# Attention scores with the keys on the partitions, and a maximum from the high halves alone

## The reference

```python
s = jnp.einsum('bqhd,bkhd->bhqk', qn, k_nope) + jnp.einsum('bqhd,bkd->bhqk', qr, k_rope)
pr = jax.nn.softmax(s.astype(jnp.float32) * scale, axis=-1).astype(v.dtype)
return jnp.einsum('bhqk,bkhd->bqhd', pr, v)
```

## Time and profile before

| | us |
|---|---|
| median of 3 runs | 1148.6 (1147.55 to 1149.5) |
| the profiled execution | 1144.88 |
| its span in the profile | 1143.1 |
| PE busy | 1117.8 (98%) |
| DVE busy | 826.1 (72%) |
| ACT busy | 555.4 (49%) |
| POOL busy | 464.2 (41%) |

### The profile page before, as it was taken

How to read it: one execution, slowest core, us unless ns; L and a number is a source line. 1 busy time by engine, 2 the same in 40 slices (tenths; PEclk the granted TensorE clock), 3 DMA queues, 4 the chain that set the end, 5 groups by cost and what they waited for, 6 DMA issues and landing times.

```text
span 1143.1 us, 15837 instructions
## 1 busy us (share of the span) xinstructions
PE 1117.8 (98%) x5146; PEld 896.6 (78%) x5146; DVE 826.1 (72%) x1170; ACT 555.4 (49%) x986; POOL 464.2 (41%) x405
## 2 busy tenths in 40 slices
PE   8999999999999989999999999999999999999996
PEld 7787766665888867888888888888888888888885
DVE  7784976674468899878787878787876757757555
ACT  6312687775223454545454545454554545533332
POOL 0185642322566046765676567655310202211000
PEclk9999999999999999999999999999999999999999
DMA  6610000104652126444544454445896565533341
GB/s 209 222 44 26 1 12 13 38 19 164 204 202 104 56 81 205 165 138 152 178 165 138 154 176 165 138 155 172 330 344 204 190 197 192 168 108 118 92 143 74
DMA packets 138431, 161.60 MB, mean 141 GB/s; under 512 B 8755, under 2 KB 105354, under 8 KB 133770
## 3 DMA queue, kind: packets, MB, share of 16 engines
q1 hardware_dynamic: 138080, 160.82, 42.0%
q10 hardware_dynamic: 298, 0.11, 0.0%
HBM read 115.55 MB, written 45.35 MB: 141 GB/s over the span
## 4 chain that ended last, share of the span: by engine, by line
PE 86%; DVE 10%; issue 2%; ACT 1%; POOL 1%; DMA 0%; DVEq 0%; SPq 0%; POOLq 0%; ACTq 0%
PE ps L298 26%; PE ps L299 26%; PE ps L300 26%; PE ps L869 2%; PE ps L850 2%; DVE WL L2050 1%; PE ps L711 1%; PE ps L861 1%; DVE XL L1727 1%; DVE SF L2149 1%; DVE SF L2157 1%; DVE WDHL L1907 1%; DVE col L1918 1%; DVE XT L1721 0%; DVE R L1900 0%
## 5 line engine op out<-in xcount | busy, mean ns | idle before, releaser
L298 PE MATMUL ps<-XH,WH 128*128 128x512 f32 x722 | 287.1, 398 | 0.8 <-DVE WL L339 0.5
L300 PE MATMUL ps<-XH,WL 128*128 128x512 f32 x722 | 281.2, 390 | 0.0
L299 PE MATMUL ps<-XL,WH 128*128 128x512 f32 x722 | 281.1, 389 | 0.0
L298 PEld LDWEIGHTS ps<-XH,WH 128*128 128x128 f32 x722 | 135.6, 188 | 32.4 <-issue 3.0
L299 PEld LDWEIGHTS ps<-XL,WH 128*128 128x128 f32 x722 | 135.7, 188 | 29.1 <-issue 2.2
L300 PEld LDWEIGHTS ps<-XH,WL 128*128 128x128 f32 x722 | 135.5, 188 | 28.5
L298 PE MATMUL ps<-GHL,WH 128*128 128x512 f32 x394 | 153.6, 390 | 0.8 <-DVE WL L2050 0.7
L300 PE MATMUL ps<-GHL,WL 128*128 128x512 f32 x394 | 153.3, 389 | 0.0
L299 PE MATMUL ps<-GHL,WH 128*128 128x512 f32 x394 | 153.3, 389 | 0.0
L334 ACT ACTIVATE WH<-WR 128x1024 fp32r<-128x1024 f32 (+3 forms) x45 | 45.5, 1011 | 138.7 <-PE ps L300 129.4
L1476 ACT ACTIVATE SF<-ps,col 128x512 f32<-128x512 f32 x88 | 68.2, 778 | 74.6 <-PE ps L300 65.6
(11 more groups left out here) (241 smaller groups left out, 2250.8 us busy)
## 6 DMA issues: line engine op xcount, KB each, us to landing
TL<-in_w_up SPq DMA_DIRECT2D x48, 256.0 KB, 3.6
s_scratch<-XT SPq DMA_DIRECT2D x11, 1024.0 KB, 4.7
XT<-in_w_down SPq DMA_DIRECT2D x11, 1024.0 KB, 6.5
t_scratch<-XT SPq DMA_DIRECT2D x11, 1024.0 KB, 3.8
WR<-t_scratch SPq DMA_DIRECT2D x44, 256.0 KB, 2.7
TL<-s_scratch SPq DMA_DIRECT2D x44, 256.0 KB, 2.9
WR<-in_w_up SPq DMA_DIRECT2D x40, 256.0 KB, 3.5
WR<-in_w_down SPq DMA_DIRECT2D x33, 256.0 KB, 3.7
```

The source lines that it names most:

```text
L298: pe.matmul(out, wh, xh, start=first, stop=False, skip_group_check=skip)
L299: pe.matmul(out, wh, xl, start=False, stop=False, skip_group_check=skip)
L300: return pe.matmul(out, wl, xh, start=False, stop=last, skip_group_check=skip)
```

## The change

The scores are made the other way round: `scores(v)` now takes 128 keys as weights and all 512 queries of the head as the moving operand. The exponentials then lie as `weigh` needs them, and ACT writes them to `XT` directly (`exponent`); the transposes, their copies and the row sums that came with the exponential are gone. The maximum of a query must be known before the first score: `rough(v)` makes a product of the high halves alone for 128 queries (one product, two banks), DVE takes its negated row maximum into `MXR`, `turn_max(n)` turns the four columns of a head into four rows with one small product, and `max_rows(n)` writes them, each masked to its own block of queries, into four more rows of `QH` (4 x 512). These rows meet ones in `KH` in the first of the three exact products, which so has 100 contraction rows. PE's step is now: `rough` of block v + 3, `scores` of block v - 2, and after every second of four steps `turn_max`.

The sums of the exponentials are added up over the four key blocks on POOL (`key_sum`, three additions per head into `SUM`); PE adds them over the partitions (`total`); DVE transposes the result in blocks of 32 x 32, takes the inverse of 16 columns, ACT spreads it over 32 columns each, DVE transposes back and scales (`inverse`, `spread_rc`, `scale_rows`). The projections and the other work are moved to other steps. POOL writes a rounded identity and the rows of ones once, early in the program. The first of the reloads of `XT` on SP also wait for the sums' product.

```diff
-            def scores(i, u):
-                j, t = divmod(u, TT)
-                s, h = divmod(j, 2)
+            def rough(v):
+                n, t = divmod(v, TT)
+                s, h = divmod(n % 4, 2)
                 if t == 0:
-                    pe.wait_ge(q_lo, i * 4 + j + 1)
-                    pe.wait_ge(k_lo, i * 4 + j + 1)
-                if i * 16 + u >= 3:
-                    pe.wait_ge(exp_done, i * 16 + u - 2)
-                tok = slice(t * P, (t + 1) * P)
-                ins = mm3(pe, s_bank(i * 16 + u)[:, :], QH[0:HEAD, s, h, tok], QL[0:HEAD, s, h, tok],
-                          KH[0:HEAD, s, h, :], KL[0:HEAD, s, h, :], True, True)
-                ins.then_inc(s_ready, 1)
-
-            def turn(i, u):
-
-                pe.wait_ge(exp_done, i * 16 + u + 1)
-                if i == 0 and u < 2:
-                    pe.wait_ge(v_copied, u + 1)
+                    pe.wait_ge(q_hi, n + 1)
+                    pe.wait_ge(k_hi, n + 1)
+                if v >= 2:
+                    pe.wait_ge(max_ready, v - 1)
+                pe.matmul(m_bank(v)[:, :], QH[0:HEAD, s, h, t * P:(t + 1) * P], KH[0:HEAD, s, h, :],
+                          start=True, stop=True).then_inc(m_ready, 1)
+
+            def turn_max(n):
+
+                pe.wait_ge(max_ready, 4 * n + 4)
+                if n:
+                    pe.wait_ge(max_row, n)
                 else:
-                    pe.wait_ge(pt_ready, i * 16 + u - 1)
-                for k in range(TT):
-                    ins = pe.transpose(ps[4 + u % 2][:, k * P:(k + 1) * P], p_buf(i * 16 + u)[:, k * P:(k + 1) * P], ident[:, :])
-                ins.then_inc(p_tr, 1)
+                    pe.wait_ge(k_lo, 2)
+                    pe.wait_ge(consts_set, 4)
+                pe.matmul(ps[1][0:TT, 0:P], MXR[:, n % 2, 0:TT], ident_r[:, :], start=True, stop=True).then_inc(max_turned, 1)
+
+            def scores(v):
+                n, k = divmod(v, TT)
+                s, h = divmod(n % 4, 2)
+                if k == 0:
+                    pe.wait_ge(max_row, n + 1)
+                    pe.wait_ge(q_lo, n + 1)
+                    pe.wait_ge(k_lo, n + 1)
+                if v < 2:
+                    pe.wait_ge(v_copied, v + 1)
+                else:
+                    pe.wait_ge(exp_done, v - 1)
+                keys = slice(k * P, (k + 1) * P)
+                o = s_bank(v)[:, :]
+                pe.matmul(o, KH[0:MAXED, s, h, keys], QH[0:MAXED, s, h, :], start=True, stop=False)
+                pe.matmul(o, KH[0:HEAD, s, h, keys], QL[0:HEAD, s, h, :], start=False, stop=False)
+                pe.matmul(o, KL[0:HEAD, s, h, keys], QH[0:HEAD, s, h, :], start=False, stop=True).then_inc(s_ready, 1)
 
...
+            def total(i, s):
+
+                pe.wait_ge(sum_step, 3 * (i * 4 + 2 * s + 2))
+                if i or s:
+                    pe.wait_ge(rr_copied, i * 2 + s)
+                pe.wait_ge(v_copied, i * 2 + s + 1 + (i < HEADS // 2 - 1) * (2 - s))
+                for h in range(2):
+                    ins = pe.matmul(ps[7][h * V_DIM:(h + 1) * V_DIM, :], ones[:, 0:V_DIM], SUM[2 * s + h], start=True, stop=True)
+                ins.then_inc(rr_ready, 1)
+
             def pair(i, last):
                 for u in range(4 * TT):
-                    turn(i, u)
-                    if u + 3 < 4 * TT:
-                        scores(i, u + 3)
-                    elif not last:
-                        scores(i + 1, u + 3 - 4 * TT)
+                    v = 4 * TT * i + u
+                    if v + 3 < 2 * HEADS * TT:
+                        rough(v + 3)
+                    if v >= 2:
+                        scores(v - 2)
+                    if u % TT == 1:
+                        turn_max(v // TT)
...
-            for u in range(3):
-                scores(0, u)
+            for v in range(3):
+                rough(v)
...
-            def exponent(i, u):
-
-                act.wait_ge(max_ready, i * 16 + u + 1)
-                if i and u % 8 == 0:
-                    act.wait_ge(rc_ready, i * 2 - 1 + u // 8)
-                act.activation(p_buf(i * 16 + u), s_bank(i * 16 + u)[:, :], ACT.Exp,
-                               bias=col[:, NB + u % 4:NB + u % 4 + 1],
-                               accum_out=col[:, RS + u:RS + u + 1]).then_inc(exp_done, 1)
-
...
+            def exponent(v):
+
+                n, k = divmod(v, TT)
+                act.wait_ge(s_ready, v + 1)
+                if v in (8, 12):
+                    act.wait_ge(d_lo, 7 if v == 8 else 8)
+                    act.wait_ge(keep_lo, 3 if v == 8 else 6)
+                if k == 0 and n >= 4:
+                    act.wait_ge(o_ready, n // 2 - 1)
+                    act.wait_ge(sum_step, 3 * (n - 3))
+                act.activation(PT[:, (n + 2) % 4, k, :], s_bank(v)[:, :], ACT.Exp).then_inc(exp_done, 1)
+
+            def spread_rc(i, s):
+
+                act.wait_ge(rc_ready, 2 * (i * 2 + s) + 1)
+                act.activation(RT.rearrange("p (b c) -> p b c", c=32), col[:, RC:RC + 16].unsqueeze(2).broadcast_to([P, 16, 32]),
+                               ACT.Copy).then_inc(o_hi, 1)
...
                         if u == 2:
                             keep(4)
                         if u == 3:
+                            q_split(0, 2)
+                            keep(1)
                             act.wait_ge(rot_done, 6)
                             split_w_hi(act, T_ATT, q_proj, 4, cols=4)
                         if u == 4:
-                            q_split(0, 3)
...
-            def maximum(i, u):
-                dve.wait_ge(s_ready, i * 16 + u + 1)
-                dve.tensor_reduce(col[:, NB + u % 4:NB + u % 4 + 1], s_bank(i * 16 + u)[:, :], AX_X, ALU.max,
-                                  negate=True).then_inc(max_ready, 1)
+            def maximum(v):
+                n, k = divmod(v, TT)
+                dve.wait_ge(m_ready, v + 1)
+                dve.tensor_reduce(MXR[:, n % 2, k:k + 1], m_bank(v)[:, :], AX_X, ALU.max, negate=True).then_inc(max_ready, 1)
+
+            def max_rows(n):
+                s, h = divmod(n % 4, 2)
+                dve.wait_ge(max_turned, n + 1)
+                if n >= 4:
+                    dve.wait_ge(s_ready, 4 * (n - 3))
+                dve.tensor_tensor(QH[HEAD:MAXED, s, h, :].rearrange("p (a q) -> p a q", a=TT),
+                                  ps[1][0:TT, 0:P].unsqueeze(1).broadcast_to([TT, TT, P]),
+                                  ident[0:TT, 0:TT].unsqueeze(2).broadcast_to([TT, TT, P]), ALU.mult).then_inc(max_row, 1)
 
             def inverse(i, s):
-                dve.wait_ge(exp_done, i * 16 + 8 * (s + 1))
-                if i:
-                    dve.wait_ge(dr_ready, i * 2 + s - 1)
-                dve.reciprocal(col[:, RC + 8 * s:RC + 8 * s + 8], col[:, RS + 8 * s:RS + 8 * s + 8]).then_inc(rc_ready, 1)
+                n = i * 2 + s
+                dve.wait_ge(rr_ready, n + 1)
+                dve.transpose(RT, ps[7][:, :]).then_inc(rr_copied, 1)
+                dve.wait_ge(rr_copied, n + 1)
+                dve.reciprocal(col[:, RC:RC + 16].unsqueeze(2), RT.rearrange("p (b c) -> p b c", c=32)[:, :, 0:1]).then_inc(rc_ready, 1)
 
             def scale_rows(i, s):
-                dve.wait_ge(o_ready, i * 2 + s + 1)
-                dve.wait_ge(rr_copied, i * 2 + s + 1)
+                n = i * 2 + s
+                dve.wait_ge(o_hi, 2 * n + 1)
+                dve.transpose(RB[:, :], RT).then_inc(rc_ready, 1)
+                dve.wait_ge(o_ready, n + 1)
+                dve.wait_ge(rc_ready, 2 * n + 2)
                 dve.tensor_tensor(RB[:, :], ps[6][:, :], RB[:, :], ALU.mult).then_inc(o_norm, 1)
...
+                    v = 4 * TT * i + u
+                    if v + 2 < 2 * HEADS * TT:
+                        maximum(v + 2)
+                    if u % TT == 2:
+                        max_rows(v // TT)
                     if i:
                         if u == 0:
+                            scale_rows(i - 1, 0)
+                        if u == 1:
+                            q_low(i, 1)
+                        if u == 2:
+                            k_low(i, 1)
+                        if u == 3:
+                            output(i - 1, 0)
...
+            def key_sum(n, k):
+
+                a, buf = PT[:, (n + 2) % 4], SUM[n % 4]
+                pool.wait_ge(exp_done, 4 * n + k + 1)
+                if k == 1:
+                    if n >= 4:
+                        pool.wait_ge(rr_ready, n // 2 - 1)
+                    pool.tensor_tensor(buf, a[:, 0, :], a[:, 1, :], ALU.add).then_inc(sum_step, 1)
+                else:
+                    pool.wait_ge(sum_step, 3 * n + k - 1)
+                    pool.tensor_tensor(buf, buf, a[:, k, :], ALU.add).then_inc(sum_step, 1)
```

278 lines of the change are left out of this document (131 added, 147 removed).

## The result

The changed kernel takes **1178.55 us** (median of four runs, 1177.77 to 1179.42) against 1148.07 (1147.04 to 1149.5) for the kernel before on the same chip: 1.0265 times, 95% interval 1.0247 to 1.0283. It is slower, as forecast, but by 30.5 us instead of 4.3, far outside the range. The profiled span is 1176.0 against 1143.1 us.

A forecast was written before the change was run, and what follows sets the result against it. PE was taken to bound pairs 1 and 2, with DVE also full early in pair 0. Pair 0 +5.0, pairs 1 and 2 -2.6, pair 3 +0.6, after it -0.9, port +0.7, clock +1.5: +4.3, 1152.9 us; range 1144 to 1158.5.

The follow-up runs named there:

- a_last: The changed kernel with its two new SBUF tensors, ident_r and MXR, laid behind all others; 1161.53 us, 1.0144 times the kernel before.
- c_norows: a_last with exact scores from 96 contraction rows, without the maxima, whose rows are written where no product reads them; 1162.2 us.
- b_pad64: The kernel before with an unused tensor of 64 bytes a partition added behind `ones`; 1161.58 us, ratio 1.0128.
- f_late: a_last with one query split earlier, unread products at TensorE's waits, and VectorE's two output-weight splits in pair 3 seven steps later; 1157.2 us.
- c_fill: a_last with 34 unread 128x512 products put at four places where TensorE waited in pair 0; 1160.4 us, ratio 1.0108.

## What to carry to other kernels

An added tensor is a part of the change even where nothing touches it: count what its size does to the distance between the two operands of the products that bound the kernel, and put small tensors last, or pad them, if no other order is known to be free. A wait of two microseconds on TensorE can be paid twice, for itself and for the products that then run at half clock; in a_last that held for three of the four such waits at the start of pair 0 and in it, and in c_norows for the one of 2.01 us in pair 1 and not for the one of 2.00 in pair 2. And a second engine that is full in one stretch makes a cheaper TensorE worth nothing there: here 7.8 us came back from lighter maxima and nothing from a shorter way through them.

## What the runs showed of the hardware

- A product of 128x512 with weights WH moving XH starts 227 ns after the one before it if their distance is as in the kernel before or 256 or 512 bytes more, and 233 ns if it is 64 or 576 bytes more; three products with CHL and WDHL right behind such ones took the 233 too (b_pad64); the recorded 0.39 us doesn't tell it, only the starts do.
- Of four executions of f_late one kept a mean clock of 0.999 and was 4.3 us quicker than the other three.
- Granted clock 0.55 also came where TensorE had waited only 0.30 us (c_fill, 57 to 60 us), in some executions and not in others. Open.
- A product of scores next to a weighing or to sums (L872 to L884, L844 to L870 in a_last) takes 0.1 us more, on either side; ahead of transposes it did not (L300 to L850, 0.23 us in the kernel before), behind them it did (L298 to L299, 0.32).
